# Splitting a value layer norm over ScalarE, a matmul and row sums, and moving four convolution taps from GpSimd to VectorE

## The reference, cut to what matters

```python
def chunked_spatial_gating(z, ln_g, ln_b, w_s, b_s):
    u, v = jnp.split(z, 2, axis=-1)
    v = layer_norm(v, ln_g, ln_b)
    ...
    w = jnp.where(causal, w_s, jnp.zeros_like(w_s))
    mixed = jnp.einsum('hts,bcshd->bcthd', w, v) + b_s.T[None, None, :, :, None]
    return u * mixed.reshape(bn, s, A_WIDTH)

def conformer_conv(z, conv_w, conv_b, ln_g, ln_b):
    a, g = jnp.split(z, 2, axis=-1)
    h = a * jax.nn.sigmoid(g)
    h = causal_dwconv(h, conv_w, conv_b)      # 31 taps along the tokens
    h = layer_norm(h, ln_g, ln_b)
    return jax.nn.silu(h)
```

## Time and profile before

| | us |
|---|---|
| median of 3 runs | 2411.16 (2410.75 to 2412.59) |
| the profiled execution, its own time | 2408.87 |
| its span, first to last instruction | 2407.1 |
| TensorE busy in the span | 2348.3 (98%) |
| VectorE busy | 1348.5 (56%) |
| ScalarE busy | 936.6 (39%) |
| GpSimd busy | 1123.0 (47%) |
| mean granted clock of TensorE | 0.989 |

### The profile page before, as it was taken

How to read it: one execution, slowest core, us unless ns; L and a number is a source line. 1 busy time by engine, 2 the same in 40 slices (tenths; PEclk the granted TensorE clock), 3 DMA queues, 4 the chain that set the end, 5 groups by cost and what they waited for, 6 DMA issues and landing times.

```text
span 2407.1 us, 33622 instructions
## 1 busy us (share of the span) xinstructions
PE 2348.3 (98%) x11781; PEld 1911.1 (79%) x11781; DVE 1348.5 (56%) x2132; ACT 936.6 (39%) x1495; POOL 1123.0 (47%) x529
## 2 busy tenths in 40 slices
PE   7999999999999999999999999999999999999998
PEld 6777788888776778888888678888888968888886
DVE  6786777772448651111158857263567474736455
ACT  3467332222336733222244544222256383322222
POOL 2346354554536535444446534444454473444443
PEclk9999999999999999999999999999999999999999
DMA  7530446653322023322332132323232202232322
GB/s 292 205 123 2 158 169 213 247 209 114 113 71 71 28 70 105 96 96 96 96 100 94 53 105 90 104 87 104 88 121 92 92 19 79 88 105 88 105 87 79
DMA packets 70095, 262.01 MB, mean 109 GB/s; under 512 B 7904, under 2 KB 8416, under 8 KB 68960
## 3 DMA queue, kind: packets, MB, share of 16 engines
q1 hardware_dynamic: 66816, 251.01, 30.8%
q10 hardware_dynamic: 3168, 9.50, 1.1%
HBM read 258.38 MB, written 2.10 MB: 108 GB/s over the span
## 4 chain that ended last, share of the span: by engine, by line
PE 88%; DVE 5%; issue 2%; POOL 1%; DMA 1%; ACT 1%; POOLq 1%; DVEq 0%; SPq 0%; ACTq 0%
PE bank L718 26%; PE bank L720 26%; PE bank L719 26%; PE bank L890 2%; PE bank L909 2%; PE bank L878 2%; POOL w_lo L640 1%; DMA first_mods<-in_first 1%; DVE acc L1646 1%; POOLq L706 1%; DVE bank L2254 1%; POOL prob L658 1%; PE bank L820 0%; DVE bank L1906 0%; DVE prob L1825 0%
## 5 line engine op out<-in xcount | busy, mean ns | idle before, releaser
L640 POOL TENSOR_TENSOR w_lo<-raw,w_hi 128x1024 fp32r<-128x1024 f32 x378 | 943.9, 2506 | 1178.9 <-ACT w_hi L1233 1176.9
L718 PE MATMUL bank<-h_hi,w_hi 128*128 128x512 f32 x1760 | 695.4, 395 | 12.3 <-DVE h_lo L1693 7.8
L719 PE MATMUL bank<-h_lo,w_hi 128*128 128x512 f32 x1760 | 688.9, 391 | 0.0
L720 PE MATMUL bank<-h_hi,w_lo 128*128 128x512 f32 x1760 | 688.9, 391 | 0.0
L1233 ACT ACTIVATE w_hi<-raw 128x1024 fp32r<-128x1024 f32 x378 | 392.6, 1051 | 426.8 <-PE bank L720 387.3
L718 PE MATMUL bank<-g_hi,w_hi 128*128 128x512 f32 x1072 | 421.1, 393 | 0.0
L720 PE MATMUL bank<-g_hi,w_lo 128*128 128x512 f32 x1072 | 420.9, 393 | 0.0
L719 PE MATMUL bank<-g_lo,w_hi 128*128 128x512 f32 x1072 | 417.3, 389 | 0.0
L718 PEld LDWEIGHTS bank<-h_hi,w_hi 128*128 128x128 f32 x1760 | 333.0, 189 | 93.4 <-DVE h_lo L1693 8.7
L720 PEld LDWEIGHTS bank<-h_hi,w_lo 128*128 128x128 f32 x1760 | 332.7, 189 | 70.4
L719 PEld LDWEIGHTS bank<-h_lo,w_hi 128*128 128x128 f32 x1760 | 333.2, 189 | 69.2 <-issue 0.8
(11 more groups left out here) (295 smaller groups left out, 2461.0 us busy)
## 6 DMA issues: line engine op xcount, KB each, us to landing
raw<-in_panels SPq DMA_DIRECT2D x378, 512.0 KB, 3.5
modraw<-in_blocks SPq DMA_DIRECT2D x80, 512.0 KB, 3.7
first_mods<-in_first SPq DMA_DIRECT2D x4, 2048.0 KB, 21.9
x<-in_x SPq DMA_DIRECT2D x1, 2048.0 KB, 8.3
w<-in_w ACTq DMA_DIRECT2D x1, 2048.0 KB, 8.7
out<-yout ACTq DMA_DIRECT2D x8, 256.0 KB, 2.2
mask<-in_causal ACTq DMA_DIRECT2D x1, 1024.0 KB, 5.0
mask<-in_dilated ACTq DMA_DIRECT2D x1, 1024.0 KB, 7.5
```

Of the source, the lines that this page charges most:

```text
L640: pool.tensor_tensor(w_lo[:, slot, :], raw[:, slot, :], w_hi[:, slot, :].bitcast(F32), ALU.subtract)\
L718: pe.matmul(out, w_h, m_h, start=start, stop=False)
L719: pe.matmul(out, w_h, m_l, start=False, stop=False)
L720: return pe.matmul(out, w_l, m_h, start=False, stop=stop)
```

## The change

- **Value norm.** The eight instructions of VectorE go. VectorE makes one small instruction, minus mean times inverse deviation, and raises `vnorm_ready`. ScalarE then does four instructions over 128x512 (scale and bias per token), after the second set of taps behind the value panels, and raises `vln_ready`.
- **Gain and bias of the norm.** The gain is folded into the bias addition of the mix, which becomes a `scalar_tensor_tensor` with four columns of a new constant. The norm's bias needs the row sums of the masked mix matrices: TensorE makes them with 8 products of 64x128x128 into bank 7 after `rstd(3)`, two layers' stages earlier, and VectorE adds them, times the bias, into `bs` with four instructions over 128x128 before the FFN of the second layer. For that the causal mask is moved on GpSimd from before the panels `P_AG` to after the fourth panel of the second layer's output projection. The constant `rows` shrinks from three rows to one.
- **Chunk 1 of the convolution.** GpSimd has 22 taps in place of 26. VectorE's 8 are summed in bank 4 after chunk 3's copy has left it, and one more instruction adds the two parts at the very end. `conv_taps` takes chunk 1 along with the others.
- **Counts.** One tap fewer after each pair of value panels.

```diff
-TAPS_WITH = {P_TAP + _n: taps for _n, taps in enumerate((2, 2, 2, 2, 2, 4, 2, 4, 4, 2))}
+TAPS_WITH = {P_TAP + _n: taps for _n, taps in enumerate((2, 2, 2, 2, 2, 2, 2, 2, 2, 4))}
...
-        TAP_BANK = (7, None, 6, 5)
+        TAP_BANK = (7, 4, 6, 5)
...
-            split_from(P_OUT1 + RING, P_AG - P_OUT1 - RING)
+            split_from(P_OUT1 + RING, 4)
             pool.wait_ge(layer2_landed, 48)
             pool.affine_select(out=wsT[:, :, :], in_=wsT[:, :, :], compare_op=ALU.is_ge, fill=0.0, base=0,
                                pattern=[[0, 8], [1, P]], channel_multiplier=-1).then_inc(ws_masked, 1)
-            split_from(P_AG, P_TAP + RING - P_AG)
+            split_from(P_OUT1 + RING + 4, P_TAP - P_OUT1 - 4)
...
             rstd(3)
+            pe.wait_ge(ws_masked, 1)
+            for c in range(4):
+                for b in range(2):
+                    m = pe.matmul(bank[7][HD * b:HD * b + HD, P * c:P * c + P], ones[:, 0:HD], wsT[:, 2 * c + b, :],
+                                  start=True, stop=True)
+            m.then_inc(ws_summed, 1)
             ffn(1, P_FFN1, 3)
...
                 split_hi(P_U + c + RING)
                 make_taps(P_U + c)
+                if c == 0:
+                    act.wait_ge(vnorm_ready, 1)
+                    for j in range(QB):
+                        m = act.activation(v2t[:, j, :], v2t[:, j, :], ACT.Identity, bias=lnst[:, j, 10:11],
+                                           scale=lnst[:, j, 9:10])
+                    m.then_inc(vln_ready, 1)
...
             norm_h(3)
+            dve.wait_ge(ws_summed, 1)
+            for c in range(4):
+                dve.scalar_tensor_tensor(out=bs[:, c, :], in0=bank[7][:, P * c:P * c + P], scalar=col("vlnb", c),
+                                         in1=bs[:, c, :], op0=MUL, op1=ADD)
             ffn(1, P_FFN1, 3)
...
-                    part = cout[:, 1, :] if c == 1 else bank[TAP_BANK[c]][:, :]
-                    if c == 1 and k == 1 + POOL_TAPS:
-                        dve.wait_ge(tap_added, POOL_TAPS)
+                    part = bank[TAP_BANK[c]][:, :]
...
+                    if c == 1 and k == 1 + POOL_TAPS:
+                        dve.wait_ge(chunk3_ready, 1)
+                        dve.tensor_scalar(part, pad[:, c, k:k + T], col("cconv", 4 * k + c), None, MUL)
+                        continue
...
-                conv_taps(18 if p == P_V2 else 5, (0, 2, 3))
+                conv_taps(17 if p == P_V2 else 4, (0, 2, 3))
...
-            for j in range(QB):
-                dve.scalar_tensor_tensor(out=v2t[:, j, :], in0=v2t[:, j, :], scalar=lnst[:, j, 6:7], in1=rows[:, 1, :],
-                                         op0=SUB, op1=MUL)
-            dve.drain()
-            for j in range(QB):
-                dve.scalar_tensor_tensor(out=v2t[:, j, :], in0=v2t[:, j, :], scalar=lnst[:, j, 9:10], in1=rows[:, 2, :],
-                                         op0=MUL, op1=ADD)
-            dve.drain()
-            dve.sem_inc(vln_ready, 1)
+            dve.scalar_tensor_tensor(out=lnst[:, :, 10:11], in0=lnst[:, :, 6:7], scalar=-1.0, in1=lnst[:, :, 9:10],
+                                     op0=MUL, op1=MUL).then_inc(vnorm_ready, 1)
...
                 if c < 3:
-                    conv_taps(4, (0, 2, 3))
+                    conv_taps(4, (0, 2, 3, 1))
...
-                dve.tensor_tensor(ysp[:, c % 2, :].rearrange("p (j t) -> p j t", j=QB),
-                                  bank[(P_U + c) % RING][:, :].rearrange("p (j t) -> p j t", j=QB),
-                                  bs[:, c:c + 1, :].broadcast_to((P, QB, P)), ADD).then_inc(bias_added, 1)
-                conv_taps(1, (0, 2, 3) if left[3] else (1,))
+                dve.scalar_tensor_tensor(out=ysp[:, c % 2, :].rearrange("p (j t) -> p j t", j=QB),
+                                         in0=bank[(P_U + c) % RING][:, :].rearrange("p (j t) -> p j t", j=QB),
+                                         scalar=col("vlng", c), in1=bs[:, c:c + 1, :].broadcast_to((P, QB, P)),
+                                         op0=MUL, op1=ADD).then_inc(bias_added, 1)
+                conv_taps(1, (0, 2, 3, 1))
...
             mix_low(3)
-            conv_taps(2 * TAPS_CONV, (0, 2))
-            while left[3]:
-                conv_taps(1, (3,))
-                if len(left[1]) > 1:
-                    conv_taps(1, (1,))
-            conv_taps(TAPS_CONV, (1,))
+            conv_taps(4 * TAPS_CONV, (0, 2, 3, 1))
+            dve.wait_ge(tap_added, POOL_TAPS)
+            dve.drain()
+            dve.tensor_tensor(cout[:, 1, :], cout[:, 1, :], bank[TAP_BANK[1]][:, :], ADD).then_inc(conv_done, 1)
+            done.append(1)
```

More of the change, by code:

```diff
@@ L111 @@
     ("final1", KB), ("even", KB), ("bu", 4), ("bga", 4), ("bgg", 4), ("cconv", TAPS_CONV * 4), ("cconvb", 4),
-    ("clng", 4), ("clnb", 4), ("odd", KB), ("ffn2", KB), ("ffn3", KB),
+    ("clng", 4), ("clnb", 4), ("vlng", 4), ("vlnb", 4), ("odd", KB), ("ffn2", KB), ("ffn3", KB),
     ("fw2", TAPS_FFN * 2 * FC), ("fb2", 2 * FC), ("fw3", TAPS_FFN * 2 * FC), ("fb3", 2 * FC), ("final2", KB),
@@ L249, in build @@
         wsT = v("wsT", [P, 8, P], 8)
-        rows = v("rows", [P, 3, 512], 12)
+        rows = v("rows", [P, 512], 12)
         bs = v("bs", [P, 4, P], 18)
@@ L365, in build @@
         ws_masked = sem("ws_masked")
+        ws_summed = sem("ws_summed")
+        vnorm_ready = sem("vnorm_ready")
         pad_ready = sem("pad_ready")
@@ L1160, in _ @@
             pe.wait_ge(vln_ready, 1)
-            pe.wait_ge(ws_masked, 1)
             for c in range(4):
@@ L1503, in _ @@
             act.dma_start(wsT[:, :, :], A["wsT"]).then_inc(layer2_landed, 16)
-            act.dma_start(rows[:, :, :], A["rows"]).then_inc(layer2_landed, 16)
+            act.dma_start(rows[:, :], A["rows"]).then_inc(layer2_landed, 16)
             act.dma_start(bs[:, :, :], A["bs"]).then_inc(layer2_landed, 16)
@@ L2252, in conv_taps @@
                         continue
-                    whole = k == TAPS_CONV - 1 and c != 3
+                    if c == 1 and k == 1 + POOL_TAPS:
+                        dve.wait_ge(chunk3_ready, 1)
+                        dve.tensor_scalar(part, pad[:, c, k:k + T], col("cconv", 4 * k + c), None, MUL)
+                        continue
+                    whole = k == TAPS_CONV - 1 and c in (0, 2)
                     m = dve.scalar_tensor_tensor(out=cout[:, c, :] if whole else part, in0=pad[:, c, k:k + T],
                                                  scalar=col("cconv", 4 * k + c), in1=part, op0=MUL, op1=ADD)
-                    if k == TAPS_CONV - 1:
+                    if k == TAPS_CONV - 1 and c != 1:
                         if c == 3:
@@ L2286, in _ @@
                     m = dve.scalar_tensor_tensor(out=v2t[:, j, at:at + 2 * P], in0=tokens_of(p, j // 2)[:, j % 2, :],
-                                                 scalar=both_inverse[:, j:j + 1], in1=rows[:, 0, at:at + 2 * P],
+                                                 scalar=both_inverse[:, j:j + 1], in1=rows[:, at:at + 2 * P],
                                                  op0=MUL, op1=ADD)
@@ L2497, in laid_out @@
         "cconvb": c(f["even_conv_b_2"]), "clng": c(f["even_conv_ln_g_2"]), "clnb": c(f["even_conv_ln_b_2"]),
+        "vlng": c(f["even_v_ln_g_2"]), "vlnb": c(f["even_v_ln_b_2"]),
         "odd": c(f["odd_norm_g_2"]), "ffn2": c(f["ffn_norm_g_2"][0]), "ffn3": c(f["ffn_norm_g_2"][1]),
@@ L2520, in laid_out @@
     out["wsT"] = f["even_w_s_2"][0].transpose(2, 0, 1)
-    rows = np.stack([b_in[512:1024], f["even_v_ln_g_2"][0], f["even_v_ln_b_2"][0]])
-    out["rows"] = np.broadcast_to(rows, (P, 3, 512))
+    out["rows"] = np.broadcast_to(b_in[512:1024], (P, 512))
     bs = f["even_b_s_2"][0].reshape(4, 2, 1, P)
```

## The result

The changed kernel takes 2428.71 us (median of 4 runs, 2425.38 to 2430.66) against 2411.39 for the kernel before on the same chip (4 runs, 2410.75 to 2412.59): a ratio of 1.0064, 95% interval 1.0051 to 1.0076. It is 17 us slower, and outside the predicted range.

The account below looks back on a forecast made before the run. TensorE, busy 2348.3 of 2407.1 us, was taken as the bound. Chunk 1 2.1 us late, less 0.4 from low halves, gave +1.7 us at the sums of squares, carried to the 2411.16 median: 2412.9 us, range 2407.4 to 2416.5.

Parts of the forecast that it names:

- the part on what costs or gives nothing: Outside VectorE's loop: row sums, mask, small instructions, the smaller `rows` load and ScalarE's covered instructions add 0 us.
- VectorE's norm is gone; the loop starts 4.15 us earlier.: Third layer's mixer: without 14.6 us of norm, VectorE's mix loop starts at 1359.65 in place of 1363.81.
- ScalarE's part is covered.: Ahead of the mix: ScalarE's four new instructions, 2.6 us, end at about 1346.5, hidden by 12 us of cover.
- Rival 4: ScalarE's part comes after 1358.5 because GpSimd's additions hold its taps: about 2415 us; chance 0.02.
- The row sums and the mask cost nothing.: Behind `rstd(3)`, 1.09 us of row sums fit a 2.59 us hole; mask moved under 6.72 us idle: 0.
- The addition holds the last mean; chunk 1 is 2.1 us late.: End of VectorE's loop: chunk 1's addition follows the last low half, done at 1372.8, before 1370.7; the last mean waits.
- rival 1: The earlier loop reaches TensorE whole, the last low half decides, a 3.9 us move: 2407.4 us; chance 0.11.
- +1.7 us at the sums of squares.: Output projection's end: chunk 1 2.1 us late, 0.4 back from low halves; sums start at 1381.1, not 1379.43.
- Behind the sums all is as before.: After the sums of squares start, TensorE has its next work ready, so their shift moves the end equally.
- rivals, 3: The pause costs the clock throughout the 24 products; sums begin at 1384.8, +5.4: 2416.5 us; chance 0.08.
- finishing line: Start of the sums of squares, 1379.43 before; what the change moves there, it moves the end.
- Rival 2: TensorE runs its mixer work as soon as it can, gaining the whole 8.8 us: 2402.4 us; chance 0.09.

Follow-up runs that it names:

- the first experiment: The kernel before with eight unused columns in `cols`, moving every later tile up 64 bytes: 2427.86 us, ratio 1.0049 to the kernel before.
- experiment 2: The whole change with its eight constants behind the columns of `rows`, so no tile moves, against the kernel before: 2414.2 us, ratio 1.0002.
- experiment 6: The whole change, constants behind `rows`, `g` tiles 192 bytes higher, against the kernel before: 2412.16 us, ratio 0.9994.
- experiment 7: As experiment 6, with VectorE's last five taps beside the panels of `u` and chunk 1's addition ahead of the loop: 2401.17 us, 0.9949 of the kernel before.
- experiment 4: The kernel before with only the `g` tiles moved, 192 bytes higher: 2407.55 us, ratio 0.9976 to the kernel before.

## Why the prediction was wrong

**The step that failed** is the part on what costs or gives nothing, in what it says of constants: "The load of `rows` gets smaller and is waited for by nobody in that stretch." It looked at constants as loads only, and it passed over the eight new columns of `cols` entirely. They cost no load and no instruction that matters, but 64 bytes of place for every later tile, and that was the largest term of the sum: +15.7 us by the starts, 14.9 by the first experiment. The forecast's sum had no term for products outside the mixer, and none of its rivals had either, so the range could not reach it. Nor could a row of the trace of before have priced it by itself; but its page did show that the products of `g_hi` (393) and `g_lo` (389) differ for the same shape, at an idle time of zero. That was a question to ask (and it is not answered yet; see the last section).

**The mixer, point by point.** Times are taken from the first mean, 1357.55 before and 1362.73 after, to be free of the shift.

- *VectorE's norm is gone; the loop starts 4.15 us earlier.* The first bias addition comes 2.16 us after the first mean, before 6.26: 4.1. Right.
- *ScalarE's part is covered.* It ends at 1351.8, and the mix starts at 1363.7. The cover is 11.9 us (12 forecast). The row of ScalarE shows 2.92 us, where 2.6 was forecast. Rival 4 falls.
- *The row sums and the mask cost nothing.* The row sums lie in the hole behind `rstd(3)`, which still ends on the normed input. TensorE's timeline of the changed kernel:

```profile
886.59 1.97 PE L1101 MATMUL bank<-wsT,ones 128*64 128x128 f32 x16
889.25 0.79 PE L720 MATMUL bank<-h_hi,w_hi 128*128 128x512 f32 x1 [0.69 <-DVE h_lo L1706]
```

- *The addition holds the last mean; chunk 1 is 2.1 us late.* The mean starts 15.26 us after the first one, before 13.18: +2.1. Right, and rival 1 falls by it.
- *+1.7 us at the sums of squares.* 23.37 against 21.88: +1.5. Right.
- *Behind the sums all is as before.* Wrong: too low. From the sums to the spread it takes 9.54 us at a mean granted clock of 0.64; in the kernel before the same stretch took 7.49 at 0.83. The clock explains it: products 0.63 us long, as the earlier trace rows have them at the lower level, run from 1391.35 to 1394.34, and the sums take 3.11 + 1.84. With these 2.05 us the mixer's cost in the profiled execution is 3.5. Of the rivals, 3 named the clock, but put the loss ahead of the sums; there the lower level ended as forecast, with rows of 0.39 us from 1381.53 on.

So for the instructions of the change the forecast of +1.7 us came true at the sums of squares, but those sums are not the finishing line that it took them for. From the first mean to the first column sums behind the mixer the kernel before takes 73.79 us at a mean granted clock of 0.93. The change takes 77.37 at 0.89 in the changed kernel, 77.15 at 0.89 in experiment 2 and 73.72 at 0.93 in experiment 6: what it costs in the end, between nothing and 3.6 us in these three executions, goes with the level of the clock behind the sums. The medians have 1.2 (experiment 2) and 4.6 (experiment 6). Rival 2, TensorE as soon as it can, was priced at 2402.4 and dismissed for the five taps in the loop; experiment 7 takes them out of the loop and, with the better place of `g`, comes to 2401.17. Without the 5.4 us of that place it would be about 2406.6, an estimate: about half of rival 2's 8.8 us. (Rival 1's 2407.4, the lower end of the range, should be 2407.3 by its own 3.9 us; nothing hangs on that.)

## What to carry to other kernels

A constant that is added in front of other tiles moves all of them: before costing a change, list which tiles get a new address, and put new constants last, or pad them so that later tiles keep their place. Where TensorE runs back to back, compare the mean time of products of one shape by their streamed tile; if they differ with no idle time before them, move one of the tiles by 64, 128 and 192 bytes and measure. Here the best of the four places for the whole kernel was the one at which streamed tiles and weights start at the same address modulo 256 bytes, which was worth 5.4 us at no cost; it was the worst for the 384 products with swapped roles, so it is no rule for every product. And an engine's freed time is worth something only where it is put in front of what waits: five taps and the addition, moved from the loop to beside the panels, gave 6.5 us in the traces, and the panels ended no later (the first mean at 1359.03, against 1358.99).

## What was not expected of the hardware

The time of a product of 128x512 depends on the distance of the streamed tile from the weights in SBUF: 226.7 ns from start to start at a distance of 0 modulo 256 bytes, 229.0 at 64, 233.1 at 128 and 233.3 at 192, the last for `g` and `h` alike. That 256 is the period is borne out at 0 as well: by the sizes of the tiles between them `h_hi` lies 49152 bytes ahead of `w_hi`, an even multiple of 256, and in experiment 4 `g_hi` lies 64768 bytes behind, an odd one, and they take 227.0 and 226.7.

The distance is not all. 229.0 is a mean of two paces: at 64 bytes the next start comes 230.1 and 229.9 ns after a product that streams `g_hi`, but 226.9 after one that streams `g_lo`, at the same distance; at the other three distances the groups differ by 0.5 ns at most. And the products of 256 columns with swapped roles have their fastest place at 64. Why is open.

It is not the writing of the weights beside it: in the changed kernel the products of `g` start 233.1 ns apart while neither ScalarE nor GpSimd is writing a weight tile (1168 pairs), and 233.0 while GpSimd is (1526 pairs). What is left is the load of the next weights that runs beside each product; that these two reads get into each other's way is the likely reading and was not tried by itself, nor were distances that are no multiple of 64 bytes.
